# Loading x from the ScalarE queue behind the bias columns, and issuing GpSimd's parameter loads ahead of its constants

## What is computed

```python
cond = jax.nn.silu(c)
h = x
for layer in range(DEPTH):
    ada = cond @ w_ada[layer] + b_ada[layer]
    sh_m, sc_m, g_m, sh_f, sc_f, g_f = jnp.split(ada, 6, axis=-1)
    u = modulate(rmsnorm(h, norm_mix[layer]), sh_m, sc_m)
    if layer < N_A_LAYERS:
        mix = forgetting_attention(u, w_in_a[layer], b_f_a[layer], ...)   # first: proj = u @ w_in
    ...
    h = h + g_m[:, None, :] * mix
    u = modulate(rmsnorm(h, norm_ffn[layer]), sh_f, sc_f)
    h = h + g_f[:, None, :] * moe_ffn(u, ...)
```

## Time and profile before

| | before |
|---|---|
| runs | 1633.71, 1630.77, 1642.31 us; median 1633.71 us |
| the profiled execution | 1633.71 us, of which 1632.0 us are the span of its trace |
| instructions | 21147 |
| busy, share of the span | PE 1502.4 us (92%), DVE 423.5 us (26%), ACT 277.2 us (17%), POOL 21.6 us (1%) |
| HBM read | 509.92 MB, 313 GB/s over the span |
| granted TensorE clock, mean | 0.952 of full |

### The profile page before, as it was taken

One profiled execution on the slowest core, in us unless ns is written; L12 is line 12 of the kernel. 1 busy time (PEld: TensorE's weight loads), 2 busy tenths in 40 slices (PEclk: granted clock), 3 DMA queues, 4 the chain that ended last, 5 costly groups with the idle time before them and its releaser, 6 DMA issues.

```text
span 1632.0 us, 21147 instructions
## 1 busy us (share of the span) xinstructions
PE 1502.4 (92%) x8561; PEld 891.6 (55%) x8561; DVE 423.5 (26%) x977; ACT 277.2 (17%) x530; POOL 21.6 (1%) x76
## 2 busy tenths in 40 slices
PE   6899897999999999999697969879999999999997
PEld 3777786455444444444385847776444444444442
DVE  0565522211111111111367348321111111111112
ACT  2211413011111111111222226321111111111110
POOL 4000000000000000000000000000000000000000
PEclk9999988999999999999798778789999999999999
DMA  9978321599999999999889800022899998999993
GB/s 343 421 310 316 148 78 59 218 379 421 420 421 359 374 421 411 420 412 421 328 346 381 323 29 1 26 85 98 348 422 422 420 393 339 423 410 421 412 421 160
DMA packets 71315, 512.38 MB, mean 314 GB/s; under 512 B 8176, under 2 KB 8400, under 8 KB 9264
## 3 DMA queue, kind: packets, MB, share of 16 engines
q1 hardware_dynamic: 70272, 509.64, 76.9%
q0 software_dynamic: 800, 1.28, 0.5%
q10 hardware_dynamic: 144, 0.08, 0.0%
HBM read 509.92 MB, written 1.05 MB: 313 GB/s over the span
## 4 chain that ended last, share of the span: by engine, by line
PE 84%; DVE 6%; ACT 6%; issue 2%; DMA 2%; SPq 0%; DVEq 0%; ACTq 0%
PE PS L795 22%; PE PS L785 13%; PE PS L442 12%; PE PS L803 12%; PE PS L818 11%; ACT scratch L993 2%; PE PS L846 2%; PE PS L612 2%; DMA ring<-in_w_ada_units 2%; PE PS L400 1%; DVE acc L523 1%; PE PS L465 1%; PE PS L885 1%; PE PS L599 1%; PE PS L479 1%
## 5 line engine op out<-in xcount | busy, mean ns | idle before, releaser
L795 PE MATMUL PS<-ring,scratch 128*32 128x512 f32 (+2 forms) x2048 | 367.9, 594 | 1.4 <-ACT scratch L993 1.4
L795 PEld LDWEIGHTS PS<-ring,scratch 128*32 128x32 f32 (+2 forms) x2048 | 117.8, 127 | 243.2 <-issue 241.4
L785 PEld LDWEIGHTS PS<-scratch,u 128*128 128x128 f32 x1664 | 194.4, 191 | 62.1 <-issue 37.6
L785 PE MATMUL PS<-scratch,u 128*128 128x128 f32 x1664 | 212.3, 281 | 12.5 <-ACT scratch L993 12.5
L442 PE MATMUL PS<-ring,uT 128*128 128x256 f32 x960 | 217.9, 387 | 2.7 <-ACT uT L413 1.5
L442 PEld LDWEIGHTS PS<-ring,uT 128*128 128x128 f32 x960 | 184.7, 194 | 29.6 <-ACT uT L413 2.1
L803 PE MATMUL PS<-ring,scratch 128*32 128x512 f32 (+2 forms) x1024 | 192.7, 611 | 2.6 <-ACT scratch L1007 1.4
L818 PE MATMUL PS<-scratch 128*128 128x512 f32 x416 | 191.6, 603 | 0.0
L1113 DVE TENSOR_TENSOR scratch<-scratch,PS 128x256 f32<-128x256 f32 x52 | 21.9, 421 | 518.9 <-ACT scratch L1002 518.9
L1120 DVE COPY scratch<-PS 128x512 f32<-128x512 f32 x104 | 71.9, 692 | 321.6 <-PE PS L803 321.6
L818 PEld LDWEIGHTS PS<-scratch 128*128 128x128 f32 x416 | 75.4, 189 | 114.6 <-issue 81.8
(11 more groups left out here) (305 smaller groups left out, 911.0 us busy)
## 6 DMA issues: line engine op xcount, KB each, us to landing
ring<-in_w_exp SPq DMA_DIRECT2D x384, 1024.0 KB, 12.5
ring<-in_w_ada_units SPq DMA_DIRECT2D x56, 1024.0 KB, 10.0
ring<-in_w_in_a_units SPq DMA_DIRECT2D x12, 1024.0 KB, 15.0
ring<-in_w_cmp_units SPq DMA_DIRECT2D x8, 1024.0 KB, 7.6
ring<-in_w_sh_units SPq DMA_DIRECT2D x6, 1024.0 KB, 17.3
ring<-in_w_kv_b_units SPq DMA_DIRECT2D x6, 1024.0 KB, 9.9
ring<-in_w_o_a_units SPq DMA_DIRECT2D x4, 1024.0 KB, 7.1
ring<-in_w_in_b_units SPq DMA_DIRECT2D x4, 1024.0 KB, 17.7
```

The source lines that it names most:

```text
L785: mm = pe_.matmul(PS[:, GATHER, i * w:(i + 1) * w], u[:, t, k * P:(k + 1) * P], hot[:, t, :], start=(t == 0), stop=(t == NT - 1))
L795: mm = pe_.matmul(PS[i * w:(i + 1) * w, GU, :], x[:, kk, i * w:(i + 1) * w], gate_and_up, start=(kk == 0), stop=(kk == KC - 1))
```

## The change

The two loads of x leave the head of SP's queue and are issued by ACT, behind `columns` and ahead of the wait for it. The 21 constants of lines 1242 to 1271 move behind the 17 parameter loads on POOL; `ones` stays first. No instruction is added or taken away.

```diff
@@ SP
-            for t in range(NT):
-                sp.dma_start(h[:, t, :], a["x"][0, t * P:(t + 1) * P, :]).then_inc(x_loaded, 16)
             units(RING[0:U_EXPERTS[0]])
@@ POOL
             done(pool.memset(ones[:, :], 1.0), ones_ready)
-            done(pool.memset(ident[:, :], 0.0))
-            done(pool.memset(causal[:, :], 0.0))
-            ...
-            done(pool.affine_select(out=block_diag[:, :], in_=block_diag[:, :], compare_op=ALU.is_ge, fill=0.0,
-                                    base=NB - 1, pattern=[[NB, H]], channel_multiplier=-1))
             pool.dma_start(pos_i[:, :], a["positions"].rearrange("o (t p) -> p (o t)", p=P),
                            allow_slow_non_contiguous=True).then_inc(params, 16)
             ...
             pool.dma_start(w_forget[:, :, :], a["w_forget"]).then_inc(params, 16)
             pool.dma_start(w_gates[:, :, :], a["w_gates"]).then_inc(params, 16)
 
+            done(pool.memset(ident[:, :], 0.0))
+            done(pool.memset(causal[:, :], 0.0))
+            ...
+            done(pool.memset(four_rows[:, :], 0.0))
+            for row in range(0, P, 32):
+                done(pool.affine_select(out=four_rows[:, :], in_=four_rows[:, :], compare_op=ALU.not_equal, fill=1.0,
+                                        base=-row, pattern=[[0, 1]], channel_multiplier=1),
+                     sem("ident_ready") if row == 96 else None)
+            ...
             done(pool.memset(row_of_pair[:, :], 0.0))
@@ ACT
             act.dma_start(columns[:, :], a["columns"]).then_inc(columns_loaded, 16)
+            for t in range(NT):
+                act.dma_start(h[:, t, :], a["x"][0, t * P:(t + 1) * P, :]).then_inc(x_loaded, 16)
             act.wait_ge(columns_loaded, 16)
```

More of the change, by code:

```diff
@@ L1241, in _ @@
             done(pool.memset(ones[:, :], 1.0), ones_ready)
+            pool.dma_start(pos_i[:, :], a["positions"].rearrange("o (t p) -> p (o t)", p=P),
+                           allow_slow_non_contiguous=True).then_inc(params, 16)
+            for dst, src in ((gain_qa, "qnorm_a"), (gain_ka, "knorm_a"), (gain_qb, "qnorm_b"),
+                             (bias_f, "b_f_a"), (bias_gate, "b_gate_b")):
+                pool.dma_start(dst[:, :], rows(a[src][0])).then_inc(params, 16)
+            for i in range(3):
+                pool.dma_start(gain_kb[:, i, :], rows(a["knorm_b"][i])).then_inc(params, 16)
+            for i in range(2):
+                pool.dma_start(bias_router[:, i, :], rows(a["b_router"][i])).then_inc(params, 16)
+            for i, name in enumerate(("pe_cmp_k", "pe_cmp_v")):
+                for half in range(2):
+                    pool.dma_start(pe[half * CMP:(half + 1) * CMP, i, :], a[name]).then_inc(params, 16)
+            pool.dma_start(w_forget[:, :, :], a["w_forget"]).then_inc(params, 16)
+            pool.dma_start(w_gates[:, :, :], a["w_gates"]).then_inc(params, 16)
             done(pool.memset(ident[:, :], 0.0))
@@ L1271, in _ @@
                                     base=NB - 1, pattern=[[NB, H]], channel_multiplier=-1))
[L1272 to L1285, removed]
             done(pool.memset(row_of_pair[:, :], 0.0))
```

## The result

| | before | after |
|---|---|---|
| median of 22 runs each | 1636.92 us | 1646.89 us |
| lowest, highest | 1630.38, 1645.46 us | 1637.04, 1654.83 us |
| span of the profiled execution | 1632.0 us | 1647.2 us |

The ratio is 1.0058, with a 95% interval of 1.0041 to 1.0077. That is 9.5 us (6.7 to 12.6) at 1637 us: a loss well inside 1%, but clear of no change, and the median lies above the forecast range, which ended at 1641.

The account below looks back on a forecast made before the run. The prediction took transfers to bound the head up to unit 3 and PE behind unit 6; the latest of four bounds put unit 7 at 34.2 us, +0.3 on 1633.7, so 1634.0 us, range 1627 to 1641.

Parts of the forecast that it names:

- The formula for unit 7: Head on PE: ada unit 7 starts no sooner than 21.8 us after x is readable (X).
- the estimate of X: When x is readable for ACT: between 11.5 and 14.1 us, costing between nothing and 2.0 us.
- the part on ACT: ACT issues x behind columns: the issues cost nothing, x has 6.1 us of slack, later landing costs 0 to 2.0 us.
- a third: Byte share of x beside SP's units, from 4 KB against 8 KB rows; gave X = 14.1 us.
- the dip: Transfers at 187 GB/s in 12 to 20 us, put down to POOL's small packets; costs 4.5 us, moves to about 5 to 13.
- the rival of turns: Mechanism of the slower rival: transfer engines serve queues in turn by packet, making x late; chance 0.2.
- the side near nothing: Choice within x's cost of nothing to 2.0 us on ACT's queue; unit 7 taken at 34.2 us, +0.3.
- the landing of w_gates: Median 13.8 us for 128 rows in the fullest stretch, said to contain a wait behind POOL's loads that x lacks.
- x late on ACT: Slower rival: x loses transfer turns on ACT's queue; 2.0 us at X = 14.1, 7.9 at 20; 1636 to 1642, chance 0.2.
- My figure of 1636: Total time in us if engines go round their queues one packet at a time, as the Trainium skill says.
- the clock: PE's clock level at turns and first projection: earlier rise about 1627 (0.13, with head gain); lower level 5.0 us more (0.07, with unseen).
- signs of being wrong: Unit 7 after 37 us; PE's units about 1.1 us before 34 us; first projection to end not about 1585 us.

Follow-up runs that it names:

- late_loads_x_on_act: late_loads with x on ACT's queue behind columns; 1639.89 us against 1637.76 for the kernel before, ratio 0.9999.
- late_loads: Kernel before with 16 of POOL's small loads issued only after five units and w_forget on ACT's queue; 1636.61 us against 1637.76, ratio 0.9986.
- x_only: Kernel before with only x moved to ACT's queue behind columns, POOL's list unchanged; 1641.31 us against 1639.01, ratio 1.0019.
- pool_only: Changed kernel with x back at the head of SP's queue, POOL's loads still ahead of the constants; 1639.70 us against 1639.01, ratio 0.9999.
- ident_early: Changed kernel with ident and four_rows made ahead of POOL's parameter loads; one run, 1640.53 us against 1639.01.
- x_only_half_rows: x_only with SP loading each of ada units 0 to 7 as two transfers of 4 KB rows; one run, 1641.59 us.
- late_loads_again: late_loads measured a second time, same kernel; 1635.65 us against 1638.67 for the kernel before, ratio 0.9980.

## Why the prediction was wrong

**What held.** Transfers are saturated and the order of their bytes doesn't change their sum: 9.85 MB by 31 us against 9.87. `ident_ready` came at 13.9 us (13.8 forecast) and was hidden. `consts` and the parameters cost nothing. ACT's two more issues were hidden in the wait for columns, though those landed 1.35 us later (6.14 against 4.79). The formula for unit 7 held too: X + 21.8 was forecast, X + 20.9 measured; 0.7 us of the difference is PE's pace of 2.81 us and not 2.94, because parts and sums overlap by 0.13.

**The step that failed** is the estimate of X, 11.5 to 14.1 us, in the part on ACT. Measured: 19.82. Three things were wrong in it.

First, I took a third as the least share that x could have. I had named the mechanism, turns by packet, but counted it in bytes of a row (4 against 8 KB) and left out the packets of columns, nine on each engine, which stand in front of x in its new queue, and the one that ends each load (x has 18 packets on each engine, not 16). Without any of POOL's loads X is at 13.74 (late_loads_x_on_act), where a third of 402 GB/s from 2.0 us on would give 9.8. That is 3.9 us of error, though 13.74 is still within the range. Unit 7 is then 0.7 us behind the kernel before (34.66 against 33.92, as X is hidden up to 13.0), but 6.7 us behind late_loads (27.93).

Second, I took the dip as a rate (187 GB/s, of which x keeps its share). It is a third queue, whose packets are small but whose turns are long. The DMA view of the kernel before, from 12 to 20 us, has it (packets, MB, share of 16 engines):

```profile
q0 software_dynamic: 183, 0.14, 54.1%
q1 hardware_dynamic: 195, 1.36, 44.3%
```

That is 0.541 x 8 x 16 / 183 = 0.38 us for each packet, against 0.29 us for one of SP's, and nearly as many packets of either queue, one in turn: with that the trace of before did speak for the rival of turns, where the prediction says that it neither proves nor excludes it. I had read only the megabytes. The dip was priced at 4.3 us of X (14.1 - 9.8), and POOL's early loads cost 6.1 (19.82 - 13.74). The two errors, 3.9 and 1.8 us, make up the 5.7 by which 19.82 lies above the latest X of the forecast.

Third, I took the side near nothing of a range, by the argument that the landing of w_gates contained the queue ahead of it. So does that of x.

**The rival that came true** is "x late on ACT", with the price worked out for X = 20 (7.9 us, 1642). I gave it 0.2 and put its likeliest point at X = 14.1. At X = 19.82 the formula gives 7.7 us for unit 7 against the 6.8 measured. The page of the Trainium skill named there, DMA: Bandwidth & Descriptors, section Queues, rings and completion order, is borne out by these traces in its rule that engines go round the queues packet by packet (437 packets against 452), with what the DMA view counts as a packet, here one row. My figure of 1636 by that rule came from the wrong count of packets, not from the rule.

**What I had placed wrongly** is the clock. The forget projection took 6.98 us against 4.76, and I had put the clock's part at the first projection alone. The two together took 14.2 us in before, x_only, pool_only, ident_early, x_only_half_rows and late_loads_again, and 15.7 to 16.4 in the changed kernel and the other experiments. late_loads and late_loads_again are the same kernel and gave 15.9 and 14.2. So nearly 2 us of this kind come without any change to the kernel, and no run here says what sets them.

**The chances.** Within 1% had 0.93, and the result lies there. What failed is the range: its upper end of 1641 was made from 5.0 + 2.0 us, the clock and the rival at its mildest, where the rival's own 7.9 and the clock's share belonged. A smaller part is the base: I anchored on the median of three runs, 1633.7, and 22 runs gave 1636.92, which is 3.2 of the 12.9 us between forecast and result; on the right base the range would have ended at 1644, still below 1646.89. Two of the three signs of being wrong appeared: unit 7 after 37 us, and 1591.3 us from the first projection to the end instead of 1585.1.

## What to carry to other kernels

When a load moves to another queue, count packets, not bytes: in these traces it waited about one packet of every other busy queue for each packet in its own queue up to its end, including those of small loads in front of it. Packets of POOL's small loads, under 1 KB, took 0.38 us each in the kernel before and 0.27 in the changed one (6 to 14 us), where SP's 8 KB rows took 0.29 and 0.36; keep such loads out of a stretch that waits for big ones. And before moving a load, look at what stands behind its wait on the engine that reads it: here the repair that touched one engine only was to let ACT copy first and wait for x later.

## What the runs showed of the hardware that was not expected

- Two halves of the change cost 0.19% [-0.01, 0.38] and -0.01% [-0.19, 0.17] alone and 0.58% [0.41, 0.77] together. The waits don't add: 7.05 us of slack absorb most of the first 9.0 us of x's delay, and none of the 4.9 us that come on top.
- The two loads of x, 1.05 MB, took 4.2 us each (median) in front of SP's units and, behind columns in ACT's queue, 10.3 us beside them, without any third queue (late_loads_x_on_act), although ACT's queue held little else.
- In the changed kernel the granted-clock column reads 1.00 in every window up to 65 us, while its units up to 42.6 us take 1.93 us, the length of the lower level. In late_loads unit 2 took 1.07 us at 13.66 us and unit 3 again 1.93 at 16.14, and of all these kernels only there does the column fall ahead of 31 us, to 0.75 in 12 to 20 us and 0.50 in 20 to 31. In the head of this kernel the durations tell the level, and the column doesn't.
